# Output projections begun before their last inputs, and the last down piece of a large expert turn finished bank by bank

## The reference, cut to what matters

```
x = x + concat(attention_A(h), ssd_B(h)) @ e_w_out          # layer 0, h = rmsnorm(x) @ w_in, split
x = x + swiglu(rmsnorm(x), ff_w_gate, ff_w_up, ff_w_down)
x = x + concat(rwkv7_C(h), latent_attention_D(h)) @ o_w_out # layer 1
x = x + top2_of_8_experts(rmsnorm(x))                       # FF_EXPERT = 3584
out = rmsnorm(x, final_norm)
```

## Time and profile before

| | before |
|---|---|
| median of 3 runs | 2468.03 us (2466.05 to 2471.07) |
| profiled execution, its time | 2473.28 us |
| profiled execution, its span | 2471.5 us |
| TensorE busy | 2310.0 us, 93% of the span |
| VectorE busy | 1170.7 us, 47% |
| ScalarE busy | 944.5 us, 38% |
| GpSimd busy | 118.7 us, 5% |
| mean granted TensorE clock | 0.967 of full |

### The profile page before, as it was taken

The page is one execution under the profiler, slowest core; times in us unless marked ns, Lnnn a source line. Parts: engine busy times, 40 slices in busy tenths (PEclk is TensorE's granted clock), DMA queues, the critical chain, the costliest instruction groups (busy, mean ns, idle before and its releaser), DMA issues.

```text
span 2471.5 us, 37908 instructions
## 1 busy us (share of the span) xinstructions
PE 2310.0 (93%) x15465; PEld 1967.8 (80%) x15465; DVE 1170.7 (47%) x1545; ACT 944.5 (38%) x1176; POOL 118.7 (5%) x179
## 2 busy tenths in 40 slices
PE   7998899999989888888999999999999999999995
PEld 6864878888877777655878787878778998999995
DVE  3266443223254577544478888888886000000001
ACT  4247332222242344344256767676765000000001
POOL 6011000000000000000000000000000000000000
PEclk9989899999989989999899999999999999999997
DMA  6320232332222000100189999999998877777663
GB/s 190 118 75 1 69 103 85 102 124 94 94 69 81 2 2 2 36 18 18 77 311 357 364 356 351 365 357 359 350 373 295 279 261 231 262 256 249 232 223 113
DMA packets 262116, 451.16 MB, mean 183 GB/s; under 512 B 8359, under 2 KB 148494, under 8 KB 261854
## 3 DMA queue, kind: packets, MB, share of 16 engines
q1 hardware_dynamic: 257216, 435.73, 50.7%
q0 software_dynamic: 4576, 13.41, 2.2%
q10 hardware_dynamic: 190, 0.05, 0.0%
HBM read 436.63 MB, written 12.52 MB: 182 GB/s over the span
## 4 chain that ended last, share of the span: by engine, by line
PE 86%; DVE 7%; ACT 4%; issue 2%; DMA 1%; ACTq 0%; DVEq 0%; POOLq 0%; SPq 0%; POOL 0%
PE bank L694 82%; PE bank L697 4%; DVE arena L2026 1%; DVE w_low L2026 1%; DVE slot L2026 1%; ACT w_high L1944 1%; ACT arena L1664 0%; DVE h_mix L2026 0%; DVE small L2083 0%; ACT w_high L1502 0%; DMA xs<-sum_rows_d 0%; DMA sum_rows_d<-arena,idx_now 0%; ACT arena L1534 0%; ACT slot L1673 0%; DMA vec_rows<-in_b_norm_w_dram 0%
## 5 line engine op out<-in xcount | busy, mean ns | idle before, releaser
L2026 DVE TENSOR_TENSOR w_low<-slot,w_high 128x2048 fp32r<-128x2048 f32 x172 | 393.6, 2291 | 332.1 <-ACT w_high L1502 265.6
L694 PE MATMUL bank<-arena 128*128 128x144 f32 (+6 forms) x2672 | 356.1, 298 | 8.2 <-ACT arena L1581 4.5
L694 PEld LDWEIGHTS bank<-arena 128*128 128x128 f32 (+4 forms) x2672 | 315.4, 183 | 24.7 <-issue 11.2
L694 PE MATMUL bank<-arena,slot 128*128 128x144 f32 (+4 forms) x2368 | 311.3, 302 | 9.9 <-issue 5.2
L694 PEld LDWEIGHTS bank<-arena,slot 128*128 128x128 f32 (+2 forms) x2368 | 288.0, 184 | 29.2 <-issue 22.3
L2026 DVE TENSOR_TENSOR arena<-arena,bank 128x512 f32<-128x512 f32 (+2 forms) x99 | 58.7, 593 | 529.4 <-PE bank L694 529.4
L2026 DVE TENSOR_TENSOR w_low<-arena,w_high 128x2048 fp32r<-128x2048 f32 x105 | 240.0, 2289 | 25.7 <-ACT w_high L1944 24.9
L694 PE MATMUL bank<-w_high,xg_high 128*128 128x512 f32 x560 | 227.6, 406 | 6.3 <-DVE w_low L2026 4.2
L1944 ACT ACTIVATE w_high<-slot 128x2048 fp32r<-128x2048 f32 x108 | 206.2, 1915 | 69.8 <-PE bank L694 39.2
L694 PE MATMUL bank<-h_ffn,w_high 128*128 128x512 f32 (+1 forms) x736 | 222.8, 386 | 3.1 <-DVE h_ffn L2026 3.1
L1944 ACT ACTIVATE w_high<-arena 128x2048 fp32r<-128x2048 f32 x105 | 201.1, 1920 | 61.8 <-PE bank L694 61.7
(11 more groups left out here) (368 smaller groups left out, 3346.8 us busy)
## 6 DMA issues: line engine op xcount, KB each, us to landing
slot<-in_moe_w_up_dram SPq DMA_DIRECT2D x86, 1024.0 KB, 7.2
arena<-in_moe_w_gate_dram SPq DMA_DIRECT2D x78, 1024.0 KB, 7.2
arena<-in_moe_w_down_dram SPq DMA_DIRECT2D x64, 1024.0 KB, 6.3
slot<-in_moe_w_down_dram SPq DMA_DIRECT2D x48, 1024.0 KB, 5.9
slot<-in_moe_w_gate_dram SPq DMA_DIRECT2D x34, 1024.0 KB, 5.1
arena<-in_moe_w_up_dram SPq DMA_DIRECT2D x26, 1024.0 KB, 5.7
slot<-in_e_w_in_dram SPq DMA_DIRECT2D x12, 1024.0 KB, 5.5
slot<-in_ff_w_gate_dram SPq DMA_DIRECT2D x11, 1024.0 KB, 5.1
```

What stands on the lines that cost most here:

```text
L694: return pe.matmul(o, lhsT, rhs, start=start, stop=True, skip_group_check=True)
L2026: return dve.tensor_tensor(o, a, b, op)
```

## The change

Three places are edited.

1. Even layer: TensorE gives block 0's tiles 0 to 2 the banks `acc[2]`, `acc[3]`, `acc[0]` (`head_banks`) and tile 3 the next turn bank. Between `y_sums(1)` and `y_scales(1)` it does tile 0's products for k 0 to 3, after `y_scales(1)` those of tiles 1 to 3; `out_proj` then does only the rest of block 0. VectorE makes three of the attention's low parts ahead of `gated(3)`, the scale of group 1 and the fourth low part ahead of `normed(0)`, and the low parts of mixer B after `normed(1)`. ScalarE makes mixer B's high parts after both roots.
2. Odd layer: the `attention` loop calls `head` after each of its three last steps: tile 0 with k 0 to 3, tile 0 with k 4 to 6, tiles 1 and 2 with k 0 to 6. `out_proj` does the rest.
3. Plain expert turns: the last down piece is done a bank at a time. ScalarE copies banks 0 and 1 as they are full (`early_banks`), VectorE bank 2. TensorE's transposes come in two halves, each with its own wait; ScalarE copies out the first 128 rows, VectorE the rows above. The split turns increment `early_banks` too, to keep its count.

```diff
 SLOT = 2048
+HEADED = (1, 3,)
 MAGIC = 1.5 * 2.0 ** 23
...
         ring.read = [(sem("ident_ready"), 1) if j == 0 else (sem("yT_ready"), 4 if j == 1 else 8)] * 4
+        if j in HEADED:
+            base = 0 if j == 1 else 24
+            ring.read = [(sem("x_added"), base + 3), ring.read[1], (sem("x_added"), base + 1), (sem("x_added"), base + 2)]
     else:
...
-def out_proj(base, high, waits, turn):
+def out_rows(base, high, parts, c, t, ks):
+    b = bank["x_added", base + 4 * c + t + 1]
+    now = slice(P * t, P * (t + 1))
+    for k in ks:
+        m = split_product(b[:, 0:256], (high[k][:, now], y_low[:, k, now]), [v[:, k, :] for v in parts], k == 0)
+    return m
+
+def head_banks(base):
+
+    for t, i in enumerate((2, 3, 0)):
+        bank["x_added", base + t + 1] = acc[i]
+
+def out_proj(base, high, waits, turn, first=None, begun=()):
     for c in range(4):
-        parts, here = split_slab()
-        pe.wait_ge(*here)
+        if c == 0 and first is not None:
+            parts = first
+        else:
+            parts, here = split_slab()
+            pe.wait_ge(*here)
         for t in range(NT):
...
                 pe.wait_ge(sem("part_low"), waits[t])
-            b, former = tile("x_added", base + 4 * c + t + 1)
-            pe.wait_ge(*former)
-            for k in range(KT):
-                now = slice(P * t, P * (t + 1))
-                m = split_product(b[:, 0:256], (high[k][:, now], y_low[:, k, now]), [v[:, k, :] for v in parts], k == 0)
+            done = begun[t] if c == 0 and t < len(begun) else 0
+            if not done:
+                b, former = tile("x_added", base + 4 * c + t + 1)
+                pe.wait_ge(*former)
+            m = out_rows(base, high, parts, c, t, range(done, KT))
             m.then_inc(sem("mix_full"), 1)
...
-def attention(first, score, value, done):
+def attention(first, score, value, done, head):
...
             m.then_inc(sem("probsT_full"), 1)
+        head(i - HEADS * NT)
...
     y_sums(1)
+    high = [y_high_even[:, k, :] for k in range(KT)]
+    head_banks(0)
+    parts, here = split_slab()
+    pe.wait_ge(*here)
+    pe.wait_ge(sem("part_low"), EVEN_PARTS + 4)
+    out_rows(0, high, parts, 0, 0, range(4))
     y_scales(1)
+    out_rows(0, high, parts, 0, 1, range(4))
+    pe.wait_ge(sem("y_tok_ready"), 3)
+    out_rows(0, high, parts, 0, 2, range(4))
+    b, former = tile("x_added", 4)
+    pe.wait_ge(*former)
+    out_rows(0, high, parts, 0, 3, range(4))
     pe.wait_ge(sem("yT_ready"), 4)
...
     turn = turns_of(1)
-    out_proj(0, [y_high_even[:, k, :] for k in range(KT)], [EVEN_PARTS + KT] * NT, turn)
+    out_proj(0, high, [EVEN_PARTS + KT] * NT, turn, parts, (4, 4, 4, 4))
...
-    attention(HEADS * NT, score_d, lambda h, k: v_d[:, k, HD * h:HD * (h + 1)], 4)
+    high = [v[:, :] for v in y_high_odd]
+    head_banks(24)
+    out_parts = []
+
+    def head(i):
+
+        if i == 0:
+            parts, here = split_slab()
+            out_parts.append(parts)
+            pe.wait_ge(*here)
+            pe.wait_ge(sem("part_low"), ODD_PARTS + KT - 1)
+            pe.wait_ge(sem("yT_ready"), 7)
+            out_rows(24, high, parts, 0, 0, range(4))
+        if i == 1:
+            out_rows(24, high, out_parts[0], 0, 0, range(4, KT - 1))
+        if i == 2:
+            for t in (1, 2):
+                out_rows(24, high, out_parts[0], 0, t, range(KT - 1))
+
+    attention(HEADS * NT, score_d, lambda h, k: v_d[:, k, HD * h:HD * (h + 1)], 4, head)
     pe.wait_ge(sem("yT_ready"), 8)
...
     turn = turns_of(3)
-    out_proj(24, [v[:, :] for v in y_high_odd], [ODD_PARTS + KT] * NT, turn)
+    out_proj(24, high, [ODD_PARTS + KT] * NT, turn, out_parts[0], (KT - 1, KT - 1, KT - 1))
...
                             m.then_inc(sem("out_tok_full"), 4)
+                        if j == GROUPS_E - 1 and k == half == 0:
+                            m.then_inc(sem("early_banks"), 2)
                 m.then_inc(sem("down_used"), 1)
...
                     pe.wait_ge(sem("out_tok_ready"), turn * 4 + 4)
-                for k in range(2):
-                    for d in range(KT):
-                        m = mm(acc[d // 3][:, CAP * (d % 3):CAP * (d % 3) + cap], slab[:, k, P * d:P * (d + 1)],
-                               hid_e[:, j % 2, CAP * k:CAP * k + cap], j == 0 and k == 0 and d % 3 == 0)
+                def add(d, k):
+                    return mm(acc[d // 3][:, CAP * (d % 3):CAP * (d % 3) + cap], slab[:, k, P * d:P * (d + 1)],
+                              hid_e[:, j % 2, CAP * k:CAP * k + cap], j == 0 and k == 0 and d % 3 == 0)
+
+                if j < GROUPS_E - 1:
+                    for k in range(2):
+                        for d in range(KT):
+                            m = add(d, k)
+                else:
+
+                    for i in range(3):
+                        for k in range(2):
+                            for d in range(3 * i, min(3 * i + 3, KT)):
+                                m = add(d, k)
+                        if i < 2:
+                            m.then_inc(sem("early_banks"), 1)
                 m.then_inc(sem("down_used"), 1)
...
-            pe.wait_ge(sem("outT_ready"), turn * 3 + 3)
-            for i, (rows, lo, half) in enumerate(((P, 0, 0), (P, 0, 1), (cap - P, P, 0), (cap - P, P, 1))):
+            for i, (rows, lo, half) in enumerate(((P, 0, 0), (cap - P, P, 0), (P, 0, 1), (cap - P, P, 1))):
+                if i % 2 == 0:
+                    pe.wait_ge(sem("outT_ready"), turn * 3 + 2 + half)
                 for d in range(4 * half, 4 * half + 4):
...
                 y_square(p)
-        for p in (2 * g, 2 * g + 1):
-            act.wait_ge(sem("yT_b_ready"), p + 1)
-            act.activation(y_high_even[:, 4 + p, :], yT[:, 4 + p, :], ACT.Copy).then_inc(sem("part_high"), 1)
+    for p in range(4):
+        act.wait_ge(sem("yT_b_ready"), p + 1)
+        act.activation(y_high_even[:, 4 + p, :], yT[:, 4 + p, :], ACT.Copy).then_inc(sem("part_high"), 1)
     act.wait_ge(sem("ssd_full"), HEADS)
...
             act.activation(xgT[:, 0:4, :], xg_ahead[:, 0:4, :], ACT.Copy).then_inc(sem("xg_copied"), 1)
-            act.wait_ge(sem("down_used"), turn * GROUPS_E + (10 + GROUPS_E))
-            for i in (0, 2):
-                n = min(3, KT - 3 * i)
-                act.activation(outT[:, 3 * i:3 * i + n, 0:cap], acc[i][:, 0:CAP * n].rearrange("p (a b) -> p a b", b=CAP)[:, :, 0:cap], ACT.Copy)\
+            for i in range(2):
+                act.wait_ge(sem("early_banks"), turn * 2 + (i + 1))
+                act.activation(outT[:, 3 * i:3 * i + 3, 0:cap], acc[i][:, 0:CAP * 3].rearrange("p (a b) -> p a b", b=CAP)[:, :, 0:cap], ACT.Copy)\
                     .then_inc(sem("outT_ready"), 1)
...
                 act.wait_ge(sem("out_tok_full"), turn * 4 + (i + 1))
-                rows = P if i < 2 else cap - P
-                act.activation(out_tok[0:rows, i // 2, 512 * (i % 2):512 * (i % 2) + 512],
-                               acc[i][0:rows, :], ACT.Copy, scale=gate_now[0:rows, i // 2:i // 2 + 1]).then_inc(sem("out_tok_ready"), 1)
+                half = i // 2
+                act.activation(out_tok[:, 0, 512 * half:512 * half + 512],
+                               acc[i][:, :], ACT.Copy, scale=gate_now[:, 0:1]).then_inc(sem("out_tok_ready"), 1)
...
                                      op0=ALU.mult, op1=ALU.mult).then_inc(sem("yT_b_ready"), 1)
-        for p in (2 * g, 2 * g + 1):
+
+    def normed_low():
+        for p in range(4):
             dve.wait_ge(sem("part_high"), EVEN_PARTS + 4 + p + 1)
...
     group_scale(0)
+    for k in range(3):
+        low_part(k)
     gated(3)
     low_dense(phase_splits(E_OUT)[0])
+    group_scale(1)
+    low_part(3)
     normed(0)
-    group_scale(1)
-    for k in range(4):
-        low_part(k)
     normed(1)
+    normed_low()
     low_dense(phase_splits(E_OUT)[0] + 1)
...
             dve.wait_ge(sem("down_used"), turn * GROUPS_E + (10 + GROUPS_E))
-            dve.tensor_copy(outT[:, 3:6, 0:cap], acc[1][:, 0:CAP * 3].rearrange("p (a b) -> p a b", b=CAP)[:, :, 0:cap])\
+            dve.wait_ge(sem("outT_ready"), turn * 3 + 2)
+            dve.tensor_copy(outT[:, 6:KT, 0:cap], acc[2][:, 0:CAP * 2].rearrange("p (a b) -> p a b", b=CAP)[:, :, 0:cap])\
                 .then_inc(sem("outT_ready"), 1)
...
                 dve.wait_ge(sem("out_tok_full"), turn * 4 + (i + 1))
-                rows = P if i < 2 else cap - P
-                dve.tensor_scalar(out_tok[0:rows, i // 2, 512:], acc[i][0:rows, :], gate_now[0:rows, i // 2:i // 2 + 1], None,
+                rows, half = cap - P, i // 2
+                dve.tensor_scalar(out_tok[0:rows, 1, 512 * half:512 * half + 512], acc[i][0:rows, :], gate_now[0:rows, 1:2], None,
                                   ALU.mult).then_inc(sem("out_tok_ready"), 1)
...
```

## The result

The changed kernel takes 2455.8 us (median of 5 runs, 2453.16 to 2460.16) against 2468.03 us before (median of 5, 2465.46 to 2471.07): ratio 0.9949, 95% interval 0.9934 to 0.9965, 12.2 us less. Measured again beside the last experiments it took 2453.62 us (median of 6) against 2472.12 (11 runs), ratio 0.9931 (0.9918 to 0.9944). The forecast was 2453 us, range 2448.4 to 2461.5.

What follows compares the result with a forecast made beforehand. TensorE, busy 93% of the span, was taken as the bound, so only its waits and half clock could be won. 6.6 + 5.5 + 2.9 = 15.0 us off the profiled run, adjusted to the median, gave 2453 us, range 2448.4 to 2461.5.

Steps and rivals of the forecast that it cites:

- Even projection: Even layer's output projection: 48 of block 0's 96 products may start early, so block 0 ends 6.6 us earlier.
- The bound of 8.1: Even projection: upper gain, 8.1 us, if the clock is back at 254.6, before `y_scales(1)`.
- The three early low parts cost nothing: VectorE, even layer: three `low_part` steps of 1.9 us fit in 2.10 us of waiting after the first scale.
- Odd projection: Odd layer's output projection: early products fill three waits, gain 5.5 us, 1.7 of it clock; 3.8 if the clock falls.
- Turns: Three large turns: the waits before the transposes (0.92, 0.92, 1.02 us) go, gain 2.9 us, low bound 2.0.
- what follows keeps its distance from the last transpose: Large turns: gated copies, addition of rows and next turn move up with the last transpose, keeping the 2.9 us.
- Rival 3: Loop's jump between the 144-row turns: arriving 0.9 us earlier doubles the 5.21 us stand, 9.8 saved, 2458.2 us; chance 0.04.
- The sum, 15.0: Whole kernel: even projection 6.6, odd projection 5.5 and large turns 2.9 us add to 15.0 us saved.
- Rival 2: Recurrence: part is given back later, some 12 us more at half clock costing 6 us, 2459 us; chance 0.08.
- rival 5: Recurrence: clock falls much further; 30 us more at half clock loses all 15.0, 45 gives 2475.5 us; chance 0.03.
- Rival 1: Both projections: waits are filled but half clock stays, 10.4 us saved, 2457.6 us; chance 0.18.
- Rival 4: TensorE's queue: an in-order wait, such as late `w_low`, holds `y_scales(1)` and all behind, 2466 us; chance 0.04.

Runs made afterwards that it cites:

- odd-late kernel: The changed kernel, but in the odd layer all 63 early products stand behind the value products; median 2453.46 us (5 runs).
- old-order run: The changed kernel, but VectorE and ScalarE keep the order of before at the end of mixer B; 2459.16 us, ratio 0.9959 to the kernel before.
- turns-only kernel: The kernel before with only the large turns' part of the change; 2467.26 us (12 runs), ratio 0.9983.
- spare products: The changed kernel, tile 0 starting on three low parts, plus two unused 128-column products in the wait left; 2452.26 us, ratio 0.9929 to the kernel before.

## Why the prediction was right

*Even projection, 6.6 us forecast.* The stage measures 7.5. The hand-overs came in the order and at the places that the steps gave them (forecast in brackets; the profile as a whole is 0.4 us later by then): early products 252.6 (252.1), scale products 255.3 (254.7), `normed(1)` 256.7 (256.7), last low part 260.6 (260.7), block 0's end 266.7 (267.2). The term that was off is the clock: I let it come back at 258.0, from bounds of 254.6 and 264.6; it was at half only from 252.6 to 256.0. It fell just as the early products began, and came back during `y_scales(1)`, which so took 1.4 us and not 2.04, and before the products behind it, of which I had counted six at half. The bound of 8.1 held. That the clock came back so early was luck: in the odd-late kernel, with the same even stage, it was at half for 6.8 us, and the gain was 6.7.

*The three early low parts cost nothing*: right, they took 1.86 us of a wait of 2.10, and 0.32 was left. The price if the order were wrong is the old-order run: 4.3 us of the stage.

*Odd projection, 5.5 forecast*: 5.3 measured, value products 1.1 us later relative to the transposes (3.40 us in place of 2.35 from the transposes' start), as forecast. The clock stayed up. The row decides against what I had taken from the Trainium skill's page *TensorE: Matmul & The Clock Gate*, part 4, for this place: about 1 us of transposes among 7 us of products did not let the clock fall, in nine profiles. Whether the transposes count as busy by themselves, as the page denies, these runs don't show.

*Turns, 2.9 forecast*: 2.6 measured. From the last down product to the next turn's first product (or, in the last turn, to the end of the transposes) it is 0.34, 1.12 and 1.17 us less. The step that failed is "what follows keeps its distance from the last transpose": true in two turns, not at the jump, which took 0.8 us of the first. The 16 transposes themselves went 0.2 us faster (1.75 in place of 1.97), which I had not counted. Rival 3 had the right place and too large a price (5.2).

*The sum, 15.0*: the stages give 7.5 + 5.3 + 2.6 = 15.4. That it is so near is in part luck, since 0.9 too little in the even stage stands against 0.2 and 0.3 too much in the others. Eleven runs of the changed kernel (2453.9 median) and 64 of the one before (2471.3) differ by 15.5 us in their means (15.3 with the five of the first measurement as well). The first medians are 12.2 apart, with an interval of 8.6 to 16.3 that holds 15.4. The profiled pair is 19.8 apart: these two profiles differ by 25 us of half clock outside the two stages, at 0.21 each 5 us, and 15.4 + 5 = 20.4. That is arithmetic on one pair, but the runs' table shows the same rate.

*Rival 2 and rival 5 (the recurrence's clock is made worse)*: not so. Over all runs the mean time at half clock fell by 12.8 us, and 13.7 us of half clock left the two stages by their profiles, so outside them it is about the same. Both rivals took 1 us more of half clock to cost 0.5 us (12 us cost 6, 30 cost 15), and so did the low end of the range (6 less give back 3). The runs show 0.21, so these terms were over twice too large. One of the prediction's own signs of being wrong did show, a recurrence more than 0.03 off the clock of 0.87 (it is 0.91); as the turns-only kernel has the same 0.91, it tells nothing of the change. *Rival 1*: refuted by the stage tables. *Rival 4*: no such wait.

Open: what lets the clock fall at 252.6 in the even stage. Idling before it is not needed (the spare products), and no run changed the narrow work ahead of it. Why the same stage is at half for 3.4 us in one profile and 6.8 in another is open too.

## What to carry to other kernels

In front of a large product whose last inputs come late, start the sums over the inputs that are there, in banks that are free, and order the engine that makes the inputs so that the early ones come first; each half alone gave 2 to 3 us, both 7.5. Price a filled wait as the wait plus what the clock loses after it: here 3.4 us of filled waits gave 5.3 us in the odd stage, 5.9 us gave 7.5 in the even one. And compare kernels by the length of the stages edited when the clock's share in the rest moves the run by more than the edit: here a kernel with a stage 1.5 us longer had the lower median. Look at the clock within the stage as well: it alone moved the even stage by 0.9 us.

## What was not expected of the hardware

- With an arrival 1.1 us earlier at the loop's jump the stand there was 6.0 us in place of 5.2, in every kernel with the turns part; so the end of such a stand need not be a fixed time behind the arrival. It was a fixed time, 2.9 to 3.0 us, behind the start of a packet of code.
- Runs of one program differ by 9 us (2466.1 to 2475.0), and most of it goes with the granted clock, 0.966 to 0.972.
- Spare products that left TensorE no idle time over 0.35 us in the even stage did not keep the clock up.
